# Two-layer mixing network on one core: order of w_mod slabs in the head, own PSUM banks for the first four k-tiles, first weight slab split by k-tile

## What is computed

```python
silu_c, silu_cc = silu(c), silu(c_ctx)
for l in range(DEPTH):                                   # first block
    shift, scale, gate = split((silu_c @ w_mod[l] + b_mod[l])[:, None, :], 3)
    shift_c, scale_c, gate_c = split(silu_cc @ w_mod[l] + b_mod[l], 3)     # w_mod[l]: 1024 x 3072
    h  = rms_norm(x)   * g_pre[l] * (1.0 + scale)   + shift
    hc = rms_norm(ctx) * g_pre[l] * (1.0 + scale_c) + shift_c
    zc = hc @ w_in[l]                                    # w_in[l]: 1024 x 8704, the same for h
    ...   # retention, differential attention, chunk MLP, merge with w_branch_out and w_out
for l in range(DEPTH):                                   # second block: w_in_2, w_branch_2, w_out_2, w_up_2, w_down_2
    ...
```

## Time and profile before

| | us |
|---|---|
| median of three executions | 1803.93 |
| lowest | 1803.73 |
| the profiled execution, as timed | 1803.99 |
| its span, from first to last record | 1802.0 |
| PE busy in the span | 1782.7 (99%) |
| POOL busy | 1360.9 (76%) |
| ACT busy | 1047.3 (58%) |
| DVE busy | 763.7 (42%) |

### The profile page before, as it was taken

How to read it: one execution, slowest core, us unless ns; L and a number is a source line. 1 busy time by engine, 2 the same in 40 slices (tenths; PEclk the granted TensorE clock), 3 DMA queues, 4 the chain that set the end, 5 groups by cost and what they waited for, 6 DMA issues and landing times.

```text
span 1802.0 us, 25383 instructions
## 1 busy us (share of the span) xinstructions
PE 1782.7 (99%) x9224; PEld 1488.9 (83%) x9224; DVE 763.7 (42%) x1340; ACT 1047.3 (58%) x1560; POOL 1360.9 (76%) x573
## 2 busy tenths in 40 slices
PE   7999999999999999999999999999999999999998
PEld 4888888888888888888888878898888878888887
DVE  2782344843334546343337374321113665431112
ACT  4645675445677654466655666565555566746554
POOL 5867787866778877676879766778887865688886
PEclk9999999999999999999999999999999999999999
DMA  9875556754556667454647544556555654456663
GB/s 367 288 256 161 167 175 205 234 158 139 154 178 189 179 204 233 139 151 151 193 134 224 152 129 140 175 167 195 187 190 173 192 143 130 148 178 196 187 186 128
DMA packets 171409, 327.88 MB, mean 182 GB/s; under 512 B 10416, under 2 KB 15792, under 8 KB 171312
## 3 DMA queue, kind: packets, MB, share of 16 engines
q1 hardware_dynamic: 168272, 320.49, 57.6%
q10 hardware_dynamic: 3040, 6.06, 0.9%
HBM read 325.46 MB, written 1.05 MB: 181 GB/s over the span
## 4 chain that ended last, share of the span: by engine, by line
PE 67%; POOL 16%; issue 16%; ACT 0%; POOLq 0%; DVE 0%; DMA 0%; ACTq 0%; DVEq 0%
POOL wlo L525 16%; PE G L1890 15%; PE G L1892 15%; PE G L1891 15%; PE A L2596 2%; PE G L2596 2%; PE A L1890 2%; PE A L1892 2%; PE A L1891 2%; PE A L2597 1%; PE G L2597 1%; PE A L2342 1%; PE G L2364 1%; PE A L1944 1%; PE A L2227 1%
## 5 line engine op out<-in xcount | busy, mean ns | idle before, releaser
L525 POOL TENSOR_TENSOR wlo<-raw,whi 128x1024 fp32r<-128x1024 f32 (+1 forms) x568 | 1357.2, 2400 | 427.2 <-ACT whi L550 424.5
L550 ACT ACTIVATE whi<-raw 128x1024 fp32r<-128x1024 f32 (+1 forms) x568 | 593.1, 1048 | 571.6 <-PE G L1892 423.8
L1890 PE MATMUL G<-whi,hparts 128*128 128x512 f32 (+1 forms) x1472 | 582.3, 396 | 1.6 <-DVE hparts L1276 0.6
L1892 PE MATMUL G<-whi,hparts 128*128 128x512 f32 (+1 forms) x1472 | 568.2, 386 | 0.0
L1891 PE MATMUL G<-wlo,hparts 128*128 128x512 f32 (+1 forms) x1472 | 567.8, 386 | 0.0
L1890 PEld LDWEIGHTS G<-whi,hparts 128*128 128x128 f32 x1472 | 276.5, 188 | 60.3 <-issue 5.2
L1892 PEld LDWEIGHTS G<-whi,hparts 128*128 128x128 f32 x1472 | 276.4, 188 | 57.0
L1891 PEld LDWEIGHTS G<-wlo,hparts 128*128 128x128 f32 x1472 | 276.8, 188 | 50.9
L1890 PE MATMUL G<-whi,osplit 128*128 128x512 f32 x240 | 94.2, 393 | 0.0
L1892 PE MATMUL G<-whi,osplit 128*128 128x512 f32 x240 | 93.4, 389 | 0.0
L1891 PE MATMUL G<-wlo,osplit 128*128 128x512 f32 x240 | 93.4, 389 | 0.0
(11 more groups left out here) (413 smaller groups left out, 2558.6 us busy)
## 6 DMA issues: line engine op xcount, KB each, us to landing
raw<-in_w_in SPq DMA_DIRECT2D x324, 512.0 KB, 3.8
raw<-in_w_up SPq DMA_DIRECT2D x64, 512.0 KB, 3.7
raw<-in_w_down SPq DMA_DIRECT2D x64, 512.0 KB, 3.5
raw<-in_w_out SPq DMA_DIRECT2D x40, 512.0 KB, 3.9
raw<-in_w_branch_out SPq DMA_DIRECT2D x36, 512.0 KB, 4.3
modw<-in_w_mod SPq DMA_DIRECT2D x32, 512.0 KB, 5.1
raw<-in_w_branch SPq DMA_DIRECT2D x24, 512.0 KB, 3.5
modz<-in_w_mod SPq DMA_DIRECT2D x16, 512.0 KB, 10.0
```

The lines of the kernel that those rows point to most:

```text
L525: pool.tensor_tensor(wlo[:, s, :, 0:n], raw[:, s, :, 0:n], whi[:, s, :, 0:n].bitcast(F32), ALU.subtract)\
L550: act.activation(whi[:, slot, :, 0:n], raw[:, slot, :, 0:n], ACT.Copy).then_inc(hi_ready, 1)
L1890: pe.matmul(bank, hi, whi[:, slot, kk, 0:n], start=first, stop=False)
L1892: return pe.matmul(bank, lo, whi[:, slot, kk, 0:n], start=False, stop=last)
```

## The change

In SP's list `MOD_FIRST` becomes four w_mod slabs behind weight slab 3 and four behind slab 4; the three for `modw` go behind slabs 10 (one) and 11 (two). In PE's list the second eight w_mod slabs go four behind n = 3, followed by the turn of quarter 2, and four behind n = 4, followed by the wait for the copy and `mod_turn`; the turn of quarter 3 goes behind n = 5. ACT does the second copy ahead of the split of weight slab 6, and quarters 2 and 3 between and behind the splits of slabs 6 and 7.

Quarters 0 and 1 are turned a second time, into G[3] and G[2] (`turn_own`); DVE applies scale and shift there and need not wait for ACT's reads before its last operation (`first_low`). Weight slab 0 is split in two halves on ACT and POOL, one k-tile each, with semaphores of their own, and PE goes through it k-tile by k-tile (`first_part`).

```diff
-        MOD_FIRST = {(1, 1): 3, (2, 0): 1, (2, 1): 4, (0, 3): 1, (1, 3): 1, (2, 3): 1}
+        MOD_FIRST = {(1, 1): 4, (2, 0): 4, (2, 2): 1, (2, 3): 2}
...
         # gpsimd
-            low_chunks((slabs - DEPTH * LAYER_SLABS) // SLOTS + 1)
+            pool.wait_ge(first_hi, w(first_hi))
+            pool.tensor_tensor(wlo[:, 0, 0], raw[:, 0, 0], whi[:, 0, 0].bitcast(F32), ALU.subtract).then_inc(first_lo, 1)
+            pool.wait_ge(hi_ready, w(hi_ready))
+            pool.tensor_tensor(wlo[:, 0, 1], raw[:, 0, 1], whi[:, 0, 1].bitcast(F32), ALU.subtract).then_inc(lo_ready, 1)
+            low_chunk(CH, range(1, SLOTS))
+            low_chunks((slabs - DEPTH * LAYER_SLABS) // SLOTS)
...
         # scalar, first_chunks
                 mod_copy()
-                split(0)
+                act.wait_ge(raw_full[0], w(raw_full[0], 16))
+                act.activation(whi[:, 0, 0], raw[:, 0, 0], ACT.Copy).then_inc(first_hi, 1)
+                act.activation(whi[:, 0, 1], raw[:, 0, 1], ACT.Copy).then_inc(hi_ready, 1)
...
+                mod_copy()
                 for slot in range(2, 4):
                     act.wait_ge(weights_used, w(weights_used))
                     split(slot)
                     if slot == 2:
-                        mod_copy()
+                        act.wait_ge(modT_ready, w(modT_ready))
+                        stream_high(0, (2,))
                 act.dma_start(const[:, N_FIRST:], g["p_const"][:, N_FIRST:]).then_inc(consts_in, 16)
                 tables(0)
-                act.wait_ge(modT_ready, w(modT_ready))
-                for q in range(2):
-                    stream_high(0, (2 + q,))
+                stream_high(0, (3,))
+                for slot in range(2):
                     act.wait_ge(weights_used, w(weights_used))
-                    split(q)
+                    split(slot)
...
         # vector
+            def first_low(q, own):
+                a = 0 if PASSES[0][0] else 1
+                high, low = h_pairs[0][q], h_pairs[1][q]
+                dve.wait_ge(first_turned, w(first_turned))
+                for k in range(2):
+                    part = own[:, k * S:(k + 1) * S]
+                    ins = dve.tensor_scalar(part, part,
+                                            modT[:, 1, 2 * q + k, a:a + 1],
+                                            modT[:, 0, 2 * q + k, a:a + 1], ALU.mult, ALU.add)
+                link(ins)
+                dve.wait_ge(h_high, w(h_high))
+                dve.tensor_tensor(low, own.rearrange("p (k s) -> p k s", k=2), high.bitcast(F32), ALU.subtract).then_inc(h_split, 1)
...
-                        stream_low(0, (2 * half_k, 2 * half_k + 1))
+                        if half_k == 0:
+                            first_low(0, G[3])
+                            first_low(1, G[2])
+                        else:
+                            stream_low(0, (2, 3))
...
         # tensor
+            def turn_own(src, banks):
+                for q, bank in enumerate(banks):
+                    for b in range(2):
+                        k = 2 * q + b
+                        for t in range(TT):
+                            ins = pe.transpose(bank[:, b * S + t * P:b * S + (t + 1) * P], src[:, t, k * P:(k + 1) * P], ident)
+                    ins.then_inc(first_turned, 1)
...
+                def first_part():
+                    pe.wait_ge(h_split, w(h_split))
+                    pe.wait_ge(first_lo, w(first_lo))
+                    for kk in range(SLAB_K):
+                        if kk == 1:
+                            pe.wait_ge(lo_ready, w(lo_ready))
+                        for t in range(TT):
+                            cols = slice(t * P, (t + 1) * P)
+                            ins = product(G[t][:], hhi[:, kk, cols], hlo[:, kk, cols], 0, kk, CH, kk == 0, False)
+                    ins.then_inc(weights_used, 1)
...
                         turn_tokens(normed, HB_FIRST, (0, 1))
+                        turn_own(normed, [G[3], G[2]])
...
-                    part(n, c, s, c == 0)
-                    for _ in range((0, 0, 5, 3, 0, 0)[n]):
+                    if n == 0:
+                        first_part()
+                    else:
+                        part(n, c, s, c == 0)
+                    for _ in range((0, 0, 0, 4, 4, 0)[n]):
                         mod_slab(A[2])
                     if n == 3:
                         turn_tokens(normed, HB_FIRST, (2,))
+                    if n == 4:
                         pe.wait_ge(mod_copied, w(mod_copied))
                         mod_turn(A[2], modrow)
-                    if n == 4:
+                    if n == 5:
                         pe.wait_ge(modT_ready, w(modT_ready, 2))
                         turn_tokens(normed, HB_FIRST, (3,))
```

More of the change, by code:

```diff
@@ L333, in build @@
         mod_turned, modT_ready = sem("mod_turned"), sem("modT_ready")
+        first_hi, first_lo, first_turned = sem("first_hi"), sem("first_lo"), sem("first_turned")
         decay_exp, decay_built, reach_ready = (sem(n) for n in (
@@ L520, in _, with low_chunk @@
             pool.memset(wlo[:].bitcast(F32), 0.0).then_inc(lo_ready, SLOTS)
-            def low_chunk(n):
-                for s in range(SLOTS):
+            def low_chunk(n, slots=range(SLOTS)):
+                for s in slots:
                     pool.wait_ge(hi_ready, w(hi_ready))
```

## The result

The changed kernel takes 1808.2 us (median of 15 executions), the one before 1803.75: a ratio of 1.0024, 95% interval 1.0017 to 1.0031. It is slower by 4.4 us where the forecast was 1803.2, 0.75 us under the median of 1803.93 known then. It lies outside the range of 1802.4 to 1805.9. Its executions are spread over 1806.09 to 1810.79, those of before over 1803.59 to 1804.2; of each kernel one execution in a slower state (2227.12 and 2532.1 us) is left out of these ranges. The profiled one has 1808.43 around a span of 1806.2.

The account below looks back on a forecast made before the run. PE's dense products bound the kernel (busy 1782.7 of 1802.0 us). First product +0.66 and -1.41 behind it gain 0.75 us, passed through to the end: 1803.2 us from a median of 1803.93; range 1802.4 to 1805.9.

Parts of the forecast that it names:

- The own turns: Eight PE transposes between w_mod slabs 4 and 5 start the first copy (m) at 19.0 instead of 18.05: 0.97 us lost.
- The hold by POOL's first half: Behind the first copy's start m, POOL's half-size operation holds DVE's L1253; shift and scale ready at m + 2.28, not 1.54.
- Fillers and chain end together; F = 23.28: Behind copy start m: fillers to m + 4.15, chain m + 4.26; first product F at 23.28, 0.66 us later.
- Four by four: Part (0,2) starts 22.96 us after the first product instead of 24.37, 1.41 less, with both w_mod groups of four.
- The same bytes go out, so slabs behind that don't move later: Head transfers: w_mod slabs in front move weight slab 4 to 31.0, slab 5 to about 37.7; slab 6 stays at 39.1.
- SP stands behind DVE for slabs 13 and 14, which land some 3 us later, 4 us ahead of need: SP's queue: DVE starts its w_mod slabs some 3 us later, so weight slabs 13 and 14 land some 3 us later.
- Behind S nothing has slack, so it goes through to the end: From the start of part (0,2) (S, 46.24) to the kernel's end, the 0.75 us gained is kept whole.
- Rival 1: Clock stays low in the head: own transposes, matmuls and half the fillers run slow; +2.4 us, 1806.3; 12%.
- Rival 2: At the second copy POOL starts ahead of DVE's L1253, which waits 2.4 us; +1.65 us, 1805.6; 13%.
- Rival 3: Slow issues on ACT, of constants and tables in a saturated queue, make quarter 3 late; +0.86 us, 1804.0; 12%.
- Rival 4: No effect: the small gain is swallowed where PE next waits for POOL or DVE; 1803.9 us; 13%.
- Rival 5: Own transposes cheap and no hold: copy at 18.7, first product 4.15 us behind it; -1.2 us, 1802.7; 10%.

Follow-up runs that it names:

- e4: Changed kernel with the w_mod slabs that SP holds behind weight slabs 12, 13 and 15 all moved behind 15; 1805.39 us.
- e10: Changed kernel with DVE's w_mod slabs early again, slab 6 split ahead of the second copy, and constants and tables issued ahead of that; 1803.97 us.
- e9: Changed kernel with ACT issuing the constants and tables ahead of the second copy; 1805.94 us.
- e1: Changed kernel with the three w_mod slabs for DVE back behind weight slabs 7, 9 and 11; 1804.25 us.
- e12: Against the kernel before: new order only, without own banks or halved slab 0; DVE's w_mod slabs early, tables ahead of second copy, SP's two slabs behind 15; 1802.96 us.
- e13: e12 plus own banks, one turned in PE's wait for the first copy and one in place of fillers (20 left of 28); 1802.68 us.

## Why the prediction was wrong, point by point

- **The own turns**: 0.97 us forecast, 0.86 measured (copy at 18.91, 19.0 forecast). Right for this pair, in part by luck: over the seven traces with these turns and the six without, the copies are 0.64 us apart on average, and the eight transposes take anything from 1.04 to 1.91 us.
- **The hold by POOL's first half**: "shift and scale are ready at m + 2.28". L1276 took 0.91 from 20.28, ready at 21.19 = m + 2.28. Right, and the hold is shown by the half slab alone.
- **Fillers and chain end together; F = 23.28**: fillers end at 23.06, the first product is at 23.09. Right. (The terms named for the chain give m + 4.23 and not 4.26, which changes nothing.)
- **Four by four**: (0,2) at 45.95 against 46.24. Right; the signs named for the head were all there.
- **"The same bytes go out, so slabs behind that don't move later"**: wrong, and the first step that failed. The bytes are the same, but not when they may be issued. The prediction weighed each weight slab against PE's need and not whether the queue still had something to do while it waited. The first two w_mod slabs for DVE, the tables and slab 10 were what kept it at 387 to 423 GB/s from 38 to 46 us; without them it fell to 16, and 1.6 MB were missing at 46 us. This delays slab 14 together with the next step: with the hole alone (e4) the first exponential was at 64.95, with the queue full and SP still behind DVE (e10) slab 14 landed at 61.24, 1.2 us later than before.
- **"SP stands behind DVE for slabs 13 and 14, which land some 3 us later, 4 us ahead of need"**: the size was low (DVE began 5.1 us later and not 3, slab 14 landed 4.5 us later) and the need was the wrong engine's. PE uses slab 14 at 69.65 in the kernel before, but ACT splits it ahead of its evacuations and exponentials, at 60.8. The margin was 0.8 us.
- **The split of slab 6 "in time"**: in time for PE, not for the transfer that waits for its slot.
- **"Behind S nothing has slack, so it goes through to the end"**: wrong. PE already waited 0.57 us for slab 16, and from the first exponential to that slab it is 10.8 to 10.9 us in each kernel of the table but e4, where DVE held the exponentials up. PE's gain passes only if the exponentials begin earlier.
- **Rivals**: the clock did fall, but behind a wait of 3.9 us and not behind the extra transposes. Rival 1 has something for it in one place, the 1.91 us that the own turns took in e9. It rested on transposes not counting as work; with the 34 transposes in the gap the granted clock of the stretch behind was 1.00, and without them 0.57. The Trainium skill (TensorE: Matmul & The Clock Gate, Part 4: PE-mode transpose) says that transposes don't count as PE's being busy in the way that other matmuls do; here they kept the clock up, and the measurement decides. Rival 2, 13%, didn't come up in the changed kernel (L1276 took 0.17 at 42.75), but did in the three with slab 6 split first (1.08, 0.69, 1.07). Rival 3 didn't come: ACT's issues took 0.33 to 0.49 us. Rival 4 named the place, a wait of PE for POOL, and e1, e12 and e13 show that the head's gain ends in the wait for slab 16 in part (1.81, 1.13 and 1.58 us of wait instead of 0.57). Rival 5 asked for no hold, and there was one. The loss itself came by a mechanism that was no rival at all.

## What to carry to other kernels

Where the queue of transfers is full for the first 60 us (364 GB/s over the head), an order of work has two schedules: when a slab is needed, and when its successor may be issued; a list that delays the second leaves the queue empty, and a queue that issues in order stands behind a slab whose buffer isn't free; together the loss turned up 20 us later on another engine. Look for each slab's first consumer in the list that is longest behind, here ACT's split ahead of a run of other work, not at the engine that is busiest. And follow a gain past the stretch that was edited to the next wait: if an engine already waits there, ask what must move for it to pass. One profiled execution gives a place in time to some tenths of a us only: lay the profiles of kernels that share a stretch side by side before a difference there is read.

## What the hardware showed

- A DVE operation with two SBUF inputs ended only when POOL's running operation had: 1.26 us for 128x8 in halves alone, 0.91 in the changed kernel, 2.19 in the earlier trace rows, where 0.17 is what it takes by itself. Being 0.03 us late was enough.
- Behind 4 us with PE empty the clock was granted at half (0.57 in the mean of 78 to 82 us); with 34 transposes in the gap it stayed at 1.00.
- PE's pace doubles between 14 and 18 us, not at the same place in each execution: the same eight transposes took 1.04 us in e4 and 1.91 in e9.
- The kernels with weight slab 0 in halves have 2.2 to 2.35 us between the device time and the span of the profiled execution, in all fifteen executions of the changed kernel too; those without, 1.9 to 2.0. So this edit costs 0.3 us that no record shows. Why stays open.
- Open too is how much of the remaining 1 us (in the profiles e13 wins 2.06 us at the head, in the medians 1.03) an earlier slab 15 would give; it wasn't tried.
